# Hybrid mLSTM/attention encoder layer: MLP up product by one level of Strassen's scheme in three token passes, its input made in the attention rounds

## The chip, the cores and the metric

One core of one Trainium2 chip. The metric is the device time of one execution of the whole kernel in microseconds; less is better.

## What is computed

One layer over 2048 prompt tokens and 32 sample tokens, width 1024, in float32: an RMS norm and one input projection that feeds an mLSTM (4 heads, chunk by chunk) and a sliding-window attention (8 query heads); the output projection and the residual; then the MLP, which the change is about; then a gated per-layer embedding and the last norm. Cut to what matters:

```python
x = x + jnp.concatenate([h_m, o_a], axis=-1) @ w_out
x = x + jnp.square(jax.nn.relu(_rmsnorm(x, g_mlp) @ w_up)) @ w_down   # w_up 1024x4096, w_down 4096x1024
x = x + jax.nn.sigmoid(_rmsnorm(x, g_ple) @ w_ple_gate) * (p @ w_ple_proj)
```

In the mLSTM each token needs the running maximum m of its chunk recurrence; every head's row of maxima is spread to all 128 partitions by a product.

## The kernel before

There are 17 tiles of tokens: 16 of 128 and one of 32. Products of full size are made of three matmuls in a reduced float32 type: each operand is split into a high part (a rounding copy, on ACT) and a low part (the remainder, on DVE), and hi*hi, hi*lo and lo*hi are added up in PSUM (split_product, L93; its three matmuls are L98, L99 and L100).

The kernel has three stages. **The mixer** runs mLSTM rounds, one tile a round, and then attention rounds. In both, a round works on several tiles at once, each at another step (r, r-1, r-2), and each engine's program is written out in the order in which it is to run; the engines meet at semaphores. In an mLSTM round PE spreads the maxima by four products with a picking matrix (L565), four products of 4 x 128 by 4 x 128 in plain float32. DVE makes the rows of gates (L716 to L749) and the norm of the tile two rounds ahead. In an attention round PE projects q, k and v, scores, turns the scores, averages, and projects the output; DVE adds it to the residual x_sum (add, L1215 to L1218), and SP stores it as x_mid (L933).

**The MLP** (mlp_phase, L1377) starts after a barrier. It takes the tokens in two halves, of 8 and of 9 tiles. At the start of a half each tile's residual is loaded, squared and summed on ACT (sum_h, L1573), its root taken on POOL (L139, L141), scaled on DVE (scale_h, L1696), turned by 8 transposes on PE (turn_h, L1632) and split (split_h L1580, low_h L1702). The split input of the whole half stays in SBUF. Then 16 blocks of 256 columns of w_up: PE makes the up product in groups of 512 tokens (first half) or 352 (second half), two times 8 chunks of 3 matmuls each; ACT rectifies a group (L1603), DVE squares it (L1735), ACT and DVE split it (L1607, L1739); PE makes the down product, 12 matmuls of 512 columns for each tile, and DVE adds it to the accumulator (L1724). The weights of the next block are loaded by SP into two raw buffers (L1487) and split into a second slot (L1557, L1683) while the block runs: both weight tiles have two slots. The first and the last block of a half are written out, those between run in a hardware loop (blocks).

**The last stage** (ple_phase) is not touched.

Engines take their instructions strictly in order. Which operation stands behind which on ACT's and DVE's queue is so given by the order in the program, and a wait holds all that follows it.

## Time and profile before

| | us |
|---|---|
| median of 3 runs | 2839.81 (2837.72 to 2840.09) |
| profiled execution | 2839.32 |
| its span | 2837.4 |
| mixer, to the start of the MLP | 1018.7 |
| MLP, to the start of the last stage | 1538.9 |

A busy time is the sum of the time in which the engine had an instruction in work; matmuls overlap, and their ends are modelled, so the distance between the starts of two neighbours says more than their durations. PEclk and the granted clock are the share of full speed that TensorE's clock was given.

### The profile page before, as it was taken

The numbers are of one execution on the slowest core, as the hardware profiler recorded it, in microseconds if no ns is written. First come the engines' busy times: TensorE is split into PE (matmuls) and PEld (weight loads), VectorE is DVE, ScalarE is ACT, GpSimd is POOL, SyncE is SP. The second block draws the span as 40 slices with busy tenths as digits, with TensorE's granted clock in tenths as the row PEclk, the third lists the DMA queues.
The fourth block names the chain that finished last, engine by engine and source line by source line (L and its number), as shares of the span: only waits on it lengthen the run. The fifth ranks groups of instructions, "written<-read, shape, count | busy, mean of one in ns | idle before, by whom it ended". The sixth has DMA issues, their size and how long they took to land. (4 is left out here: it accounts for less than half of the span.)

```text
span 2837.4 us, 36654 instructions
## 1 busy us (share of the span) xinstructions
PE 2721.6 (96%) x14337; PEld 2322.3 (82%) x14337; DVE 1372.8 (48%) x2050; ACT 744.9 (26%) x1425; POOL 76.1 (3%) x163
## 2 busy tenths in 40 slices
PE   7999999789999969999999998899999999997998
PEld 6888888678787758888888887798989898985887
DVE  6666565554444444353443545535353535344443
ACT  4333333333333232122121222211111111113232
POOL 0000000000000010000000000000000000000010
PEclk9999999899999989999999999999999999998999
DMA  5121211532222131111111113411111111114221
GB/s 193 55 76 52 73 57 41 152 132 88 81 92 93 47 127 48 50 52 37 59 44 44 58 32 123 130 31 55 34 54 35 52 37 52 37 69 167 84 80 38
DMA packets 90431, 202.93 MB, mean 72 GB/s; under 512 B 9656, under 2 KB 47640, under 8 KB 90360
## 3 DMA queue, kind: packets, MB, share of 16 engines
q1 hardware_dynamic: 89160, 197.63, 21.3%
q0 software_dynamic: 1200, 4.33, 0.5%
q8 instruction: 48, 0.79, 0.1%
q14 instruction: 23, 0.19, 0.0%
HBM read 153.59 MB, written 48.44 MB: 71 GB/s over the span
## 5 line engine op out<-in xcount | busy, mean ns | idle before, releaser
L98 PE MATMUL f_up<-f_hT_hi,f_up_hi 128*128 128x352 f32 (+1 forms) x1280 | 451.9, 353 | 9.8 <-DVE f_hT_lo L1702 9.8
L99 PE MATMUL f_up<-f_hT_lo,f_up_hi 128*128 128x352 f32 (+1 forms) x1280 | 450.8, 352 | 0.0
L100 PE MATMUL f_up<-f_hT_hi,f_up_lo 128*128 128x352 f32 (+1 forms) x1280 | 450.4, 352 | 0.0
L1724 DVE TENSOR_TENSOR f_acc<-f_acc,f_down 128x1024 f32<-128x1024 f32 (+1 forms) x272 | 331.9, 1220 | 223.0 <-PE f_down L100 221.8
L98 PE MATMUL f_down<-f_down_hi,f_uT_hi 128*128 128x512 f32 x1088 | 425.1, 391 | 0.0
L100 PE MATMUL f_down<-f_down_hi,f_uT_lo 128*128 128x512 f32 x1088 | 424.5, 390 | 0.0
L99 PE MATMUL f_down<-f_down_lo,f_uT_hi 128*128 128x512 f32 x1088 | 424.4, 390 | 0.0
L1735 DVE TENSOR_TENSOR f_u<-f_u 128x704 f32<-128x704 f32 (+1 forms) x80 | 82.1, 1026 | 541.3 <-ACT f_u L1603 541.3
L98 PEld LDWEIGHTS f_up<-f_hT_hi,f_up_hi 128*128 128x128 f32 x1280 | 242.0, 189 | 34.3 <-issue 6.6
L1603 ACT ACTIVATE f_u<-f_up 128x704 f32<-128x704 f32 (+1 forms) x80 | 69.3, 866 | 737.2 <-PE f_up L100 737.2
L99 PEld LDWEIGHTS f_up<-f_hT_lo,f_up_hi 128*128 128x128 f32 x1280 | 242.2, 189 | 23.4
L100 PEld LDWEIGHTS f_up<-f_hT_hi,f_up_lo 128*128 128x128 f32 x1280 | 242.4, 189 | 22.6
L100 PEld LDWEIGHTS f_down<-f_down_hi,f_uT_lo 128*128 128x128 f32 x1088 | 204.8, 188 | 43.1
L98 PEld LDWEIGHTS f_down<-f_down_hi,f_uT_hi 128*128 128x128 f32 x1088 | 205.0, 188 | 42.2
L99 PEld LDWEIGHTS f_down<-f_down_lo,f_uT_hi 128*128 128x128 f32 x1088 | 204.8, 188 | 42.3
L1557 ACT ACTIVATE f_down_hi<-f_raw 128x1024 fp32r<-128x1024 f32 x64 | 68.0, 1062 | 319.9 <-DMA f_raw<-in_w_down 319.9
L98 PE MATMUL m_proj<-a_wo_hi,a_mixT_hi 128*128 128x512 f32 x272 | 111.1, 408 | 4.4 <-DVE a_mixT_lo L1185 4.4
L98 PE MATMUL e_gate_ps<-e_wg_hi,e_hT_hi 128*128 128x512 f32 x272 | 109.1, 401 | 3.9 <-DVE e_hT_lo L1963 2.2
L100 PE MATMUL m_proj<-a_wo_hi,a_mixT_lo 128*128 128x512 f32 x272 | 107.0, 393 | 0.0
L99 PE MATMUL e_gate_ps<-e_wg_lo,e_hT_hi 128*128 128x512 f32 x272 | 106.8, 393 | 0.0
L100 PE MATMUL e_gate_ps<-e_wg_hi,e_hT_lo 128*128 128x512 f32 x272 | 106.7, 392 | 0.0
L99 PE MATMUL m_proj<-a_wo_lo,a_mixT_hi 128*128 128x512 f32 x272 | 106.6, 392 | 0.0
(339 smaller groups left out, 4377.2 us busy)
## 6 DMA issues: line engine op xcount, KB each, us to landing
f_raw<-in_w_up SPq DMA_DIRECT2D x64, 512.0 KB, 3.6
f_raw<-in_w_down SPq DMA_DIRECT2D x64, 512.0 KB, 3.5
hT_hi_kept<-m_hT_hi SPq DMA_DIRECT2D x17, 512.0 KB, 4.9
hT_lo_kept<-m_hT_lo SPq DMA_DIRECT2D x17, 512.0 KB, 5.7
a_hT_hi<-hT_hi_kept SPq DMA_DIRECT2D x17, 512.0 KB, 3.6
a_hT_lo<-hT_lo_kept SPq DMA_DIRECT2D x17, 512.0 KB, 4.5
m_x<-in_x_prompt SPq DMA_DIRECT2D x16, 512.0 KB, 4.3
a_x_sum<-in_x_prompt SPq DMA_DIRECT2D x16, 512.0 KB, 3.6
```

Source lines behind the costliest of these rows:

```text
L98: eng.matmul(out, lh(k), rh(k), start=f, stop=False)
L99: eng.matmul(out, lh(k), rl(k), start=False, stop=False)
L100: ins = eng.matmul(out, ll(k), rh(k), start=False, stop=e)
L1557: act.activation(quarter(slot, n, up_hi, down_hi), raw[:, n % 2, :], ACT.Copy).then_inc(w_hi_made, 1)
L1603: act.activation(u[:, :, 0:width], up_ps[g % 2][:, :, 0:width], ACT.Relu).then_inc(rectified, 1)
L1724: dve.tensor_tensor(acc[0:t.n, n, :], acc[0:t.n, n, :], down_ps[n % 2][0:t.n, :], ALU.add).then_inc(added, 1)
L1735: dve.tensor_tensor(part, part, part, ALU.mult).then_inc(squared, 1)
```

## The change

**The up product.** The 4096 columns of w_up are taken as two halves, the 1024 rows as two halves, and the tokens in pairs of tiles. One level of Strassen's scheme (Winograd's form) makes the product of a 2x2 block matrix with another from 7 products of half size where the plain way has 8. A block now takes 128 columns from each half of w_up. Seven products of 4 chunks each are made from seven sums of the weights (or parts) and seven of the input; DVE adds their PSUM results up into the four quarters of the result. Tokens go in three passes: 6, 5 and 6 tiles, in units of two tiles (a lone tile is a unit by its even and odd tokens), with 384, 320 and 336 columns a product. The first block of each pass runs unit by unit (3, 3 and 4 groups), since the operands are made one unit ahead. POOL makes the sums of weights and of inputs, ACT and DVE split all of them. The split weights have one slot each now (up by product, down by half), and the down weights one raw buffer, which both pieces of a block pass through. The result is squared straight from the rectified sum (one instruction) and kept as uT with the two tiles of a unit interleaved, so that the down product reads its stationary at every second column. The down product itself is as before. All weights are loaded three times in place of two.

**The input.** The norm and the turning of a tile move from the MLP's start into the attention rounds, three rounds behind (r-3): ACT squares, POOL takes the root, DVE scales, PE transposes, ACT copies, SP stores the turned tile to memory (hx_kept), and the MLP's POOL queue loads it. One more round follows at the end. The store of x_mid moves behind the round's other DMAs, and the load of the residual comes one round later.

**The maxima.** DVE writes each head's row of maxima on the diagonal of a 4 x 4 x 128 array of zeros, splits it, and PE spreads all four heads with two matmuls of 512 columns in the reduced type (hi and lo, against ones) in place of four in plain float32. Three DVE operations are new (ROW_STEPS 9 to 12).

```diff
-                for h in range(HEADS):
-                    pe.matmul(wide[0:m, h, 0:m], pick[:, h, 0:m], rows[:, U, 0:m], start=True, stop=True)
+                pe.matmul(wide[0:m, :, 0:m], ones_row[:, 0:m], u_hi[:, :, 0:m], start=True, stop=False)
+                pe.matmul(wide[0:m, :, 0:m], ones_row[:, 0:m], u_lo[:, :, 0:m], start=False, stop=True)
...
-                dve.tensor_tensor_scan(rows[:, U, 0:n], zero_row[:, 0:n], rows[:, G, 0:n], m_in, ALU.add, ALU.max).then_inc(row_step, 1)
+                dve.tensor_tensor_scan(rows[:, U, 0:n], rows[:, G, 0:n], rows[:, G, 0:n], m_in, ALU.max, ALU.max).then_inc(row_step, 1)
                 dve.wait_ge(row_step, step + 7)
                 dve.tensor_tensor(m_rows[:, slot, 0:n], rows[:, B, 0:n], rows[:, U, 0:n], ALU.add).then_inc(row_step, 1)
+                dve.tensor_tensor(u_own[:, :, 0:n], pick[:, :, 0:n], rows[:, U, 0:n].unsqueeze(1).to_broadcast([HEADS, HEADS, n]), ALU.mult).then_inc(row_step, 1)
+                dve.wait_ge(row_step, step + 9)
+                dve.tensor_copy(u_hi[:, :, 0:n], u_own[:, :, 0:n]).then_inc(row_step, 1)
+                dve.wait_ge(row_step, step + 10)
+                dve.tensor_tensor(u_lo[:, :, 0:n], u_own[:, :, 0:n], u_hi[:, :, 0:n], ALU.subtract).then_inc(row_step, 1)
...
+            if exists(r - 1):
+                t = tile_at(r - 1, 1 - slot)
+                src = x_sample if t.n < P else x_prompt[token_rows(sp, t.i, P), :]
+                if exists(r - 3):
+                    all_of(sp, x_out, r - 3, 16)
+                    all_of(sp, x_scaled, r - 3)
+                sp.dma_start(x_sum[0:t.n, t.slot, :], src).then_inc(x_sum_in[t.slot], 16)
+            if exists(r - 3):
+                t = tile_at(r - 3, 1 - slot)
+                dst = hx_kept[token_rows(sp, t.i, P), :].rearrange("p (c t) -> p c t", t=P)
+                all_of(sp, hxT_sb, t.i)
+                sp.dma_start(dst[:, :, 0:t.n], hxT[:, :, 0:t.n]).then_inc(hxT_out, 16)
...
+            if exists(done.i):
+                all_of(act, added, done.i, 2)
+                if on_round(r, 3):
+                    act.wait_ge(wo_lo_made, KC)
+                act.activation(hx[0:done.n, :], x_sum[0:done.n, done.slot, :], ACT.Square, scale=D ** -0.5,
+                               accum_out=ms[0:done.n, 0:1]).then_inc(x_squared, 1)
...
+            if exists(done.i):
+                all_of(act, x_turned, done.i)
+                if exists(done.i - 1):
+                    all_of(act, hxT_out, done.i - 1, 16)
+                act.activation(hxT[:, :, 0:done.n], turned[:, :, 0:done.n], ACT.Copy).then_inc(hxT_sb, 1)
...
+        def turn_x(t):
+            all_of(pe, x_scaled, t.i)
+            for c in range(KC):
+                ins = pe.transpose(turned[:, c, 0:t.n], hx[0:t.n, c * P:(c + 1) * P], ident[0:t.n, 0:t.n])
+            ins.then_inc(x_turned, 1)
...
+            if exists(old.i):
+                all_of(pe, mix_lo, old.i, 2)
+            if exists(done.i):
+                turn_x(done)
...
+            if exists(done.i):
+                if on_round(r, 3):
+                    dve.wait_ge(gain_in, 16)
+                all_of(dve, x_rooted, done.i, 2)
+                dve.scalar_tensor_tensor(hx[0:done.n, :], x_sum[0:done.n, done.slot, :], ms[0:done.n, 2:3], gmlp[0:done.n, :],
+                                         ALU.mult, ALU.mult).then_inc(x_scaled, 1)
...
+    UNITS = [[(0, 3), (1, 4), (2, 5)], [(6, 9), (7, 10), (8,)], [(11, 13), (12, 14), (15,), (16,)]]
+    PASSES = range(len(UNITS))
+    B, A, C_, D_ = range(4)
+    BANK = [B, A, C_, D_, A, C_, D_]
+    T2, B11, T3, T1, B21, T4, B22 = range(7)
+    OPERANDS = [B11, T1, T2, B21, B22, T3, T4]
...
+            def load_up(places):
+                for f in (0, 1):
+                    sp.dma_start(up_raw[:, f], w_up[:, places[f]].rearrange("(c p) j -> p c j", p=P)).then_inc(up_in, 16)
...
+            for p in PASSES:
+                def body(b):
+                    g = block_count(p, b)
+                    last = isinstance(b, int) and b == BLOCKS - 1
+                    final = last and p == PASSES[-1]
+                    places, nxt = ([place_of(at, f) for f in (0, 1)] for at in (b, 0 if last else b + 1))
+                    if not final:
+                        reached(sp, up_lo_made, g * 7 + 7)
+                        load_up(nxt)
+                    reached(sp, down_lo_made, g * 2 + 1)
+                    load_down(places[1])
+                    if not final:
+                        reached(sp, down_lo_made, g * 2 + 2)
+                        load_down(nxt[0])
+                    yield
+
+                whole(blocks(sp, p, body))
+                for n, i in enumerate(tiles(p)):
+                    reached(sp, added, down_count(p, BLOCKS - 1, n))
+                    sp.dma_start(x_mlp[token_rows(sp, i, tokens(i)), :], acc[0:tokens(i), n, :]).then_inc(acc_out, 16)
+                sp.wait_ge(acc_out, 16 * sum(len(tiles(n)) for n in range(p + 1)))
+                if p < PASSES[-1]:
+                    load_acc(p + 1)
...
+            def stage(p, u):
+                number, w = units_ahead(p, u), unit_width(UNITS[p][u])
+                a, b = sides(p, u)
+                b11, b12, b21, b22 = by_pair(a[:, 0:HC]), by_pair(b[:, 0:HC]), by_pair(a[:, HC:KC]), by_pair(b[:, HC:KC])
+                pool.wait_ge(h_in[number % 2], h_count(number))
+                reached(pool, op_lo, number * 7)
+                if u == 0:
+                    reached(pool, u_lo, group_count(p, 0) * 4)
+                pool.tensor_tensor(t1_buf(w), b12, b11, ALU.subtract).then_inc(staged, 1)
+                pool.wait_ge(staged, number * 4 + 1)
+                pool.tensor_tensor(t2_buf(w), b22, t1_buf(w), ALU.subtract).then_inc(staged, 1)
+                pool.tensor_tensor(b12, b22, b12, ALU.subtract).then_inc(staged, 1)
+                pool.wait_ge(staged, number * 4 + 2)
+                pool.wait_ge(op_lo, number * 7 + 2)
+                pool.tensor_tensor(t1_buf(w), b21, t2_buf(w), ALU.subtract).then_inc(staged, 1)
+
+            def add_weights(g):
+                a11, a12 = up_raw[:, 0, 0:HC], up_raw[:, 0, HC:KC]
+                a21, a22 = up_raw[:, 1, 0:HC], up_raw[:, 1, HC:KC]
+                reached(pool, up_in, g * 32 + 32)
+                reached(pool, up_lo_made, g * 7)
+                pool.tensor_tensor(sums_sb[:, S1], a21, a22, ALU.add).then_inc(sums, 1)
+                reached(pool, sums, g * 4 + 1)
+                pool.tensor_tensor(sums_sb[:, S2], sums_sb[:, S1], a11, ALU.subtract).then_inc(sums, 1)
+                pool.tensor_tensor(sums_sb[:, S3], a11, a21, ALU.subtract).then_inc(sums, 1)
+                reached(pool, sums, g * 4 + 2)
+                pool.tensor_tensor(sums_sb[:, S4], a12, sums_sb[:, S2], ALU.subtract).then_inc(sums, 1)
...
+            def down_weight_hi(p, b, f):
+                reached(act, down_in, block_count(p, b) * 32 + 16 * f + 16)
+                reached(act, down_done, down_count(p, b, -1))
+                act.activation(down_hi[:, f], down_raw[:], ACT.Copy).then_inc(down_hi_made, 1)
+
+            def u_half(p, k, cols, n):
+                f, side = QUARTERS[n]
+                w = cols.stop - cols.start
+                reached(act, squared, k * 4 + n + 1)
+                act.activation(uT_hi[:, f, cols, side], part[:, PART_OF[n], 0:w], ACT.Copy).then_inc(u_hi, 1)
+
+            def take_p1(k, w):
+                reached(act, product, k * 7 + 2)
+                reached(act, u_lo, k * 4)
+                act.activation(part[:, 0, 0:w], up_ps[A][:, 0:w], ACT.Copy).then_inc(p1_sb, 1)
...
+                    if not first:
+                        down_weight_hi(p, b, 0)
+                    for u, cols in enumerate(groups(p, b)):
+                        k, w = group_count(p, b) + u, cols.stop - cols.start
+                        ahead = operands_hi(p, u + 1) if first and u + 1 < len(UNITS[p]) else iter(range(7))
+                        next(ahead)
+                        next(ahead)
+                        take_p1(k, w)
+                        if first and u == 0:
+                            down_weight_hi(p, b, 0)
+                        if first and u == 1 or not first:
+                            down_weight_hi(p, b, 1)
+                        next(ahead)
+                        next(ahead)
+                        u_half(p, k, cols, 0)
+                        u_half(p, k, cols, 1)
+                        next(ahead)
+                        u_half(p, k, cols, 2)
+                        whole(ahead)
+                        u_half(p, k, cols, 3)
+                    if not last:
+                        for q in range(7):
+                            up_weight_hi(p, b + 1, q)
...
+            def up(p, b, k, cols, u):
+                w = cols.stop - cols.start
+                g = block_count(p, b)
+                if isinstance(b, int) and b == 0:
+                    pe.wait_ge(op_lo, units_ahead(p, u) * 7 + 7)
+                for q, bank in enumerate(BANK):
+                    if u == 0:
+                        reached(pe, up_lo_made, g * 7 + q + 1)
+                    if q == 4:
+                        reached(pe, p1_sb, k + 1)
+                    reached(pe, combined, k * 7 + [-6, -2, -1, 0, 1, 2, 4][q])
+                    split_product(pe, up_ps[bank][:, 0:w], (lambda c: up_hi[:, q, c], lambda c: up_lo[:, q, c]),
+                                  (lambda c: op_hi_sb[:, q, c, cols], lambda c: op_lo_sb[:, q, c, cols]), range(HC)).then_inc(product, 1)
+
+            def down(p, b):
+                k = last_group(p, b)
+                reached(pe, down_lo_made, block_count(p, b) * 2 + 2)
+                for n, i in enumerate(tiles(p)):
+                    reached(pe, u_lo, k * 4 + (3 if place(p, i)[1] == 0 else 4))
+                    reached(pe, added, down_count(p, b, n - 2 if n >= 2 else -1))
+                    for c in range(D // NB):
+                        cols = slice(c * NB, (c + 1) * NB)
+                        ins = split_product(pe, down_ps[n % 2][0:tokens(i), cols],
+                                            (lambda f: stationary(uT_hi, f, p, i), lambda f: stationary(uT_lo, f, p, i)),
+                                            (lambda f: down_hi[:, f, cols], lambda f: down_lo[:, f, cols]), range(2))
+                    ins.then_inc(down_done, 1)
...
+            def combine(w, out, bank, other):
+                dve.tensor_tensor(part[:, out, 0:w], part[:, other, 0:w], up_ps[bank][:, 0:w], ALU.add).then_inc(combined, 1)
+
+            def square(n, w):
+                x = part[:, PART_OF[n], 0:w]
+                dve.scalar_tensor_tensor(x, x, 0.0, x, ALU.max, ALU.mult).then_inc(squared, 1)
+
+            def u_low(k, cols, n):
...
+                    if not first:
+                        down_weight_lo(p, b, 0)
+                    for u, cols in enumerate(groups(p, b)):
+                        k, w = group_count(p, b) + u, cols.stop - cols.start
+                        ahead = operands_lo(p, u + 1) if first and u + 1 < len(UNITS[p]) else iter(range(7))
+                        next(ahead)
+                        next(ahead)
+                        reached(dve, p1_sb, k + 1)
+                        combine(w, 1, B, 0)
+                        if first and u == 0:
+                            down_weight_lo(p, b, 0)
+                        next(ahead)
+                        reached(dve, product, k * 7 + 3)
+                        reached(dve, combined, k * 7 + 1)
+                        combine(w, 2, C_, 1)
+                        if first and u == 1 or not first:
+                            down_weight_lo(p, b, 1)
+                        next(ahead)
+                        reached(dve, product, k * 7 + 4)
+                        reached(dve, combined, k * 7 + 2)
+                        combine(w, 3, D_, 2)
+                        combine(w, 4, D_, 1)
+                        reached(dve, combined, k * 7 + 3)
+                        square(0, w)
+                        u_low(k, cols, 0)
+                        reached(dve, product, k * 7 + 5)
+                        combine(w, 0, A, 0)
+                        reached(dve, combined, k * 7 + 5)
+                        square(1, w)
+                        u_low(k, cols, 1)
+                        next(ahead)
+                        reached(dve, product, k * 7 + 6)
+                        combine(w, 2, C_, 2)
+                        reached(dve, combined, k * 7 + 6)
+                        square(2, w)
+                        u_low(k, cols, 2)
+                        whole(ahead)
+                        reached(dve, product, k * 7 + 7)
+                        reached(dve, combined, k * 7 + 4)
+                        combine(w, 4, D_, 4)
+                        reached(dve, combined, k * 7 + 7)
+                        square(3, w)
+                        u_low(k, cols, 3)
+                    crossing = last and p < PASSES[-1]
+                    ahead = operands_lo(p + 1, 0) if crossing else iter(range(7))
+                    weights = 0
+                    for n, i in enumerate(tiles(p)):
+                        if n == len(tiles(p)) - 1:
+                            while weights < 7 and not (last and not crossing):
+                                up_weight_lo(*((p + 1, 0) if crossing else (p, b + 1)), weights)
+                                weights += 1
+                                if weights > 1:
+                                    next(ahead)
+                            whole(ahead)
+                        add(p, b, n, i)
+                        if n < len(tiles(p)) - 2 and not (last and not crossing):
+                            up_weight_lo(*((p + 1, 0) if crossing else (p, b + 1)), weights)
+                            weights += 1
+                            if weights > 1:
+                                next(ahead)
```

## Rows read from the trace of the kernel before

**Rows 1.** The page, part 1: busy time, share of the span, instructions of each engine.
```profile
PE 2721.6 (96%) x14337; PEld 2322.3 (82%) x14337; DVE 1372.8 (48%) x2050; ACT 744.9 (26%) x1425; POOL 76.1 (3%) x163
```

**Rows 2.** Windows: stretch, length, busy time of each engine, PEclk, DMA share, GB/s.
```profile
60.00:500.00 440.00, 440.00 (x2779) 390.96 (x2778) 271.84 (x633) 158.60 (x400) 22.90 (x29) 1.00 0.18 60
552.00:1000.00 448.00, 430.65 (x2587) 344.39 (x2588) 214.06 (x414) 142.63 (x438) 1.00 (x1) 0.97 0.25 85
1100.00:1740.00 640.00, 640.00 (x2789) 522.91 (x2788) 273.97 (x283) 118.28 (x116) 0.00 (x0) 1.00 0.15 47
1740.00:1790.00 50.00, 37.52 (x175) 31.82 (x174) 30.24 (x30) 18.24 (x25) 10.74 (x20) 0.86 0.61 190
```

**Rows 3.** Timeline of PE, first and last of 57, of 47 and of 23 matmuls.
```profile
1299.84 0.39 PE L98 MATMUL f_down<-f_down_hi,f_uT_hi 128*128 128x512 f32 x1
...
1312.53 0.39 PE L100 MATMUL f_down<-f_down_hi,f_uT_lo 128*128 128x512 f32 x1
...
1999.77 0.32 PE L98 MATMUL f_up<-f_hT_hi,f_up_hi 128*128 128x352 f32 x1
...
2007.09 0.32 PE L99 MATMUL f_up<-f_hT_lo,f_up_hi 128*128 128x352 f32 x1
...
485.95 0.28 PE L99 MATMUL m_proj<-m_og_lo,m_hT_hi 128*128 128x256 f32 x1
...
488.55 0.28 PE L100 MATMUL m_proj<-m_og_hi,m_hT_lo 128*128 128x256 f32 x1
```

**Rows 4.** Timeline of PE: small products in plain float32, several merged into one row.
```profile
484.04 1.06 PE L603 MATMUL m_pair<-m_qkT 128*128 128x128 f32 x8
484.93 1.06 PE L609 MATMUL m_acc<-m_v,m_k 128*128 128x129 f32 x8
...
498.89 1.15 PE L565 MATMUL m_pair<-m_rows,m_pick 4*128 4x128 f32 x8
```

**Rows 5.** Groups of DVE and ACT by shape: busy us, mean ns, idle before.
```profile
L1683 DVE TENSOR_TENSOR f_up_lo<-f_raw,f_up_hi 128x512 fp32r<-128x512 f32 x128 | 87.5, 685 | 0.0
L1224 DVE COPY a_k_twice<-m_proj 128x256 f32<-128x256 f32 x16 | 6.8, 425 | 1.2 <-PE m_proj L100 0.3
L985 ACT ACTIVATE a_wq_hi<-a_wq_raw 128x512 fp32r<-128x512 f32 x8 | 4.4, 617 | 0.0
L992 ACT ACTIVATE a_wkv_hi<-a_wkv_raw 128x256 fp32r<-128x256 f32 x8 | 2.5, 398 | 0.0
```

**Rows 6.** Timeline of a steady MLP block: DVE's square and the ACT operation that waits for it.
```profile
1341.72 1.23 DVE L1735 TENSOR_TENSOR f_u<-f_u 128x1024 f32<-128x1024 f32 x1 [7.49 <-ACT f_u L1603]
...
1343.06 1.06 ACT L1607 ACTIVATE f_uT_hi<-f_u 128x1024 fp32r<-128x1024 f32 x1 [1.37 <-DVE f_u L1735]
```

**Rows 7.** DMA issues with us to landing; a window with one such load in it.
```profile
f_raw<-in_w_up SPq DMA_DIRECT2D x64, 512.0 KB, 3.6
f_raw<-in_w_down SPq DMA_DIRECT2D x64, 512.0 KB, 3.5
...
1349.00:1353.00 4.00, 4.00 (x20) 3.30 (x19) 3.10 (x4) 1.06 (x1) 0.00 (x0) 1.00 0.38 131
```

**Rows 8.** Timeline: the MLP's start and end; and one POOL group of 128 elements.
```profile
1018.67 0.20 POOL L148 MEMSET f_ident<- 128x128 f32 x1 [465.06 <-POOLq L1310]
...
2557.59 0.35 SPq L1816 DMA_DIRECT2D e_x<-x_after_mlp  x1
...
L150 POOL TENSOR_SCALAR_AFFINE_SELECT f_ident<-f_ident 128x128 f32<-128x128 f32 x1 | 0.3, 294 | 0.1
```

**Rows 9.** Timeline of PE: first product, and transposes, after idle times of different length.
```profile
1044.11 0.77 PE L98 MATMUL f_up<-f_hT_hi,f_up_hi 128*128 128x512 f32 x1 [6.20 <-DVE f_hT_lo L1702]
...
1047.65 0.40 PE L100 MATMUL f_up<-f_hT_hi,f_up_lo 128*128 128x512 f32 x1
...
1771.94 1.94 PE L1632 MATMUL f_up<-f_ident,f_h 128*128 128x128 f32 x8 [3.20 <-DVE f_h L1696]
...
1783.00 1.07 PE L1632 MATMUL f_down<-f_ident,f_u 128*128 128x128 f32 x8 [2.12 <-DVE f_u L1696]
```

605 lines of the change are left out of this document (259 added, 346 removed).

## The prediction

> **What bounds the kernel now.** I read the page first: PE is busy for 96% of the span, DVE for 48%, ACT for 26%, POOL for 3% [rows 1]. Then the table of windows, for the stages that the change touches: in an mLSTM stretch of 440 us PE is busy for all of it, in the attention rounds for 430.7 of 448, in the steady MLP blocks of the first half for all of 640 us [rows 2]. So PE's issue rate sets the time in all three, and whatever shortens PE's queue is worth its own length, as long as no other engine becomes late. Last the timeline, for what one matmul costs in a row of many. The mean durations of the groups overlap and don't serve; starts do. 56 intervals of 512 columns take 12.69 us, 0.2266 each; 46 of 352 take 7.32, 0.159 each; 22 of 256 take 2.60, 0.118 each [rows 3]. That is a line: 0.010 us plus 0.000423 us a column. It gives 0.172 for 384 columns, 0.145 for 320 and 0.152 for 336, the widths of the three passes.
>
> The profiled execution took 2839.32 us, span 2837.4; the median of the runs is 2839.81. My sum is made against 2839.3.
>
> **Term 1, the up product in full groups: -83.** Before, per block 96 matmuls of 512 and, in the second half, 144 of 352: 16 x (96 x 0.2266 + 144 x 0.159) = 714 us. After, per block 7 products x 12 matmuls = 84: 16 x 84 x (0.172 + 0.145 + 0.152) = 631 us.
>
> **Term 2, the down product: 0.** 12 matmuls of 512 columns for each of 17 tiles in 16 blocks, before and after: 740 us. Its stationary is now read at every second column. No row has that; weight loads sit at 0.111 us each where they bind [rows 4], so even at double cost they fit beneath 0.2266.
>
> **Term 3, the first block of each pass: +84.** There the groups are one unit (128 columns or less): 3 + 3 + 4 = 10 groups of 84 matmuls. The nearest rows are 128-wide fp32 instructions, 8 in 0.89 us, 0.111 each [rows 4]; lower bound 0.064 from the line above, upper 0.222 (a plain fp32 product of 128 columns takes two such instructions). I take 0.111: 9.3 us a group. In the same time DVE has 7 operand remainders (512 elements, 0.6 from start to start), 14 operations of 128 elements (about 0.29) and 1.2 of down weights, 9.5 us, and waits for ACT in between; so 12 us a group. From pass 2 on the second piece of the down weights also stands behind 3 MB of accumulator tiles on SP's queue. I take 124 us for the three blocks, where the widths of term 1 hold 14.5 + 12.2 + 12.8 = 39.5. At 0.064 DVE and ACT hold it anyway (-17); at 0.222 it grows by about 65.
>
> **Term 4, a new wait in each of the 45 later blocks: +168.** This decides. Before, one rectify, one square and one split of up to 1024 elements followed a group, and other groups' matmuls covered them. Now, for 384 columns, DVE has 7 additions, 4 squares and 4 splits, ACT 5 copies, in one order. Prices: DVE 256 elements 0.425, 512 0.685, so 0.555 for 384; ACT 0.398 and 0.617, so 0.51 [rows 5]. DVE to ACT and back costs 0.14 (idle 1.37 around an operation of 1.23) [rows 6]. Let T be the start of the block's first product in pass 1; one product takes 12 x 0.172 = 2.07, the seventh ends at T+14.5.
> - ACT converts the first down piece once the last down matmul is through, T+0.2 to 1.3. DVE first adds the last tile (to 1.7), then takes the remainder, to 2.8.
> - Only then does SP issue the load of the second piece into the same buffer. Alone it lands in 3.5 us; 512 KB take 1.6 us of the queues (131 GB/s over 4 us), and 1 MB of next up weights, issued at T+0.6, is ahead [rows 7]. It lands at about 7.6 (6.4 without them).
> - ACT 7.7 to 8.7; DVE's remainder 8.8 to 10.0. The fourth product was ready at 8.4; its additions stand behind this in DVE's queue.
> - Then 10 DVE operations (4 additions, 3 squares, 3 splits; 5.6), three ACT copies between square and split (1.5) and their hand-overs (0.4), less 0.4 where DVE operations overlap: 7.1. Done at 17.1.
> The first down tile needs that split: PE waits 17.1 - 14.5 = 2.6. Pass 2 has a shorter cover (12.2), only three weight remainders between its tiles so that the last addition is 0.6 later, 10 operations of 0.48: done at 16.9, wait 4.7. Pass 3: 16.5 - 12.8 = 3.7. 15 x (2.6 + 4.7 + 3.8) = 168. Bounds: with the second piece there in time, DVE could start at the fourth product (8.4, 7.1, 7.5) and the waits are 1.3, 1.6 and 1.5, 66 us; with 512-byte packets at half the byte rate the load is 3.2 us later, +144. I stay near the first figure: the queues carry the old 1 KB packets and 4 KB packets in the same 3.5 to 3.6 us, so bytes, not packets, seem to set the time, and I add a tenth.
>
> **Term 5, what stood around the MLP: -53.** Before, the MLP started at 1018.7 and its first product at 1044.1, 25.4 later [rows 8, 9]. After: the attention part ends with one more tail (square 1.24, POOL 0.75, scale 1.28, transposes 0.9, copy 0.4, store 2.0 for 32 rows, one behind the other): +5 in the mixer, in term 6. From the start of the MLP both up pieces and two tiles load (5 us), POOL makes 4 weight sums and 4 operands (no row for 512 elements; its 128-element row of 0.294 times 4 gives 1.2 each), ACT and DVE split 14 pieces: 20.5 us to the first product. -5. From the first product to the start of the next stage it was 1513.5, of which 1454 are the matmuls of terms 1 and 2: 59.5 for 13 tiles' transposes, the idle of the half boundary (12.5 of 50 us) and the end [rows 2, 8]. After, two crossings at 3 to 4 us (operands are made beside the last down product) and an end of 4: 11. -48.
>
> **Term 6, the mixer: +12.** Attention: 8 transposes a tile more on PE, 0.9 and a hand-over, 17 x 0.95 = +16. Their helpers (ACT +2.3 us a round, DVE 1.3, POOL 0.8, SP a store of 512 KB) are covered by a round of 27 us in which DVE and ACT are under half busy [rows 2]; SP's new waits stand ahead of loads that are two rounds early. If that cover fails it is 17 x 2.3 = 39. mLSTM: 8 instructions of about 1.0 us (1.15 to the end of the last) [rows 4] become two of 0.227: 17 x -0.54 = -9. DVE gets three operations of 512 elements more, 2 us a round at 62% busy [rows 2]: nothing, or 34 if it is late. The longer tail: +5.
>
> **Term 7, the clock: +20.** After PE idled for 3.20 us eight transposes took 1.94, after 2.12 us 1.07; the MLP's first 8 matmuls, after 6.20 us, took 3.54 to the ninth where 8 intervals are 1.81 [rows 9]: the lower of the clock's two levels, 1.2 GHz, and a loss of 1.7. The waits of passes 2 and 3 are long enough; I take half of 30 blocks at about 1.4.
>
> Sum: -83 + 84 + 168 - 53 + 12 + 20 = +148, so 2987. Some 0.2% (6 us) is what a measurement of this kernel can tell from nothing.
>
> **A rule against the change.** POOL now adds SBUF operands four times a block, about from T+6 to T+11, beside DVE's squares and splits; in the trace POOL does no such work, so no row bears on it. The Trainium skill, "SBUF — State Buffer" (section "SBUF: two separate sides"), says that DVE with two SBUF inputs and GpSimd share a port pair that one holds for its whole instruction while the other waits. By that rule every remainder, square and split could stand up to 1.2 us behind POOL.
>
> **Rivals.**
> - No waits, faster: ACT and DVE keep up, as the 48% and 26% suggest, and the down weights land in time. From term 4's wait below 0.5 us a block on. Then 2839.3 - 83 + 84 - 53 + 12 = 2799. For it: 15 us of DVE's work lie beside 30 of PE. Against it: even the bound with everything loaded leaves 66 us. 0.12.
> - Waits of about 1 us a block, +44 in term 4: 2843, no change. 0.03.
> - POOL and DVE exclude each other: one operation of 1.2 us in the way of the chain in each of 45 blocks, and the clock lost oftener, and some 5 us in the first groups: +80, 3067. 0.23.
> - 128-wide products at 0.222: 3052. 0.10.
> - My own sum, 2930 to 3040: 0.48. Several of the bad ends together, 3150: 0.04.
> The low end, 2860, is term 4 at its bound of 66 us with no loss of clock (2865); the high end is the port's case with slow packets. Left out of 2860 to 3110 are the faster case, the unchanged one and the last: 0.19. Faster 0.12, same 0.03, slower 0.85; the slower cases' own range is 2920 to 3110.
>
> **What would show it.** In the profile after: matmuls of 384 columns starting 0.172 apart; PE idle before the first down matmul of each block, ended by the DVE split, for 2.6, 4.7 and 3.7 us; blocks of 33.4, 30.5 and 32.8 us; DVE idle before the first addition behind the down piece's remainder, ended by ACT and that by the DMA; first blocks of 36, 39 and 49 us of up product. Blocks of 31, 26 and 29 us would refute term 4. A granted clock below 1 in passes 2 and 3 and not in pass 1 bears out term 7. A POOL addition of much more than 1.2 us, or DVE splits that last longer while POOL runs, would speak for the port.

## The result, and the profile after

The kernel after takes 3217.98 us (median of 4 runs, 3209.45 to 3220.23) where the kernel before, run beside it, takes 2839.95: a ratio of 1.1326 (95% interval 1.1309 to 1.1343). The forecast was 2987, its range 2860 to 3110. Slower was right; the size was not. In the profiled executions the span grew by 370.2 us, from 2837.4 to 3207.6, where I had summed up 148.

The page, part 1 and the row of TensorE's clock, after:

```profile
PE 2885.8 (90%) x15015; PEld 2490.5 (78%) x15015; DVE 1832.5 (57%) x2992; ACT 910.4 (28%) x1914; POOL 423.4 (13%) x401
...
PEclk9999998999999599999996999999679998998999
```

PE is no longer busy all the time (96% before [rows 1]), POOL works for 423 us where it had 76, and the clock has three holes, of 5, 6 and 6 to 7 tenths, where the three passes begin.

Windows of the kernel after: the up product of the three first blocks, then the later blocks of passes 1, 2 and 3 (length, busy time and count of PE, PEld, DVE, ACT, POOL, granted clock, DMA share, GB/s):

```profile
1061.11:1116.12 55.01, 54.35 (x253) 53.97 (x253) 28.15 (x59) 13.04 (x29) 19.62 (x18) 0.50 0.28 96
1693.26:1745.38 52.12, 51.79 (x253) 51.60 (x253) 25.64 (x59) 11.39 (x29) 17.30 (x17) 0.52 0.44 152
2277.70:2350.00 72.30, 71.97 (x337) 71.78 (x337) 27.27 (x81) 13.49 (x41) 16.40 (x18) 0.50 0.26 84
1153.74:1673.35 519.61, 468.81 (x2184) 416.98 (x2185) 314.81 (x421) 118.14 (x196) 89.39 (x56) 0.93 0.19 57
1761.65:2258.05 496.40, 411.51 (x2102) 363.84 (x2100) 297.56 (x424) 118.14 (x202) 94.53 (x60) 0.94 0.21 63
2368.84:2905.58 536.74, 469.84 (x2269) 398.33 (x2268) 315.70 (x437) 119.23 (x202) 88.60 (x56) 0.92 0.19 56
```

In the first three rows PE is hardly ever idle and yet issues a matmul of 128 columns or fewer only every 0.213 us, at a granted clock of 0.50 (the level of 1.2 GHz) from beginning to end, but for the first 2.5 us of the second row. In the other three the count times the spacing at full clock falls short of the length: there PE waits, and the clock is below 1 for some of the time. Where it waits stands in the groups by shape:

```profile
L97 PE MATMUL f_down<-f_down_hi,f_uT_hi 128*128 128x512 f32 x1024 | 447.2, 437 | 178.0 <-DVE f_uT_lo L1823 168.5 <-issue 9.5
L97 PE MATMUL f_up<-f_op_hi,f_up_hi 128*128 128x320 f32 x420 | 131.9, 314 | 23.5 <-DVE f_part L1813 23.5
L97 PE MATMUL f_up<-f_op_hi,f_up_hi 128*128 128x128 f32 x196 | 80.7, 412 | 38.2 <-DVE f_op_lo L1801 38.2
```

The first wait is term 4's, ended by the DVE split as foretold. The second lies inside the up product of pass 2, ahead of its seventh product, for a PSUM bank that DVE has still to read (1.57 us a block). The third belongs to the first blocks, most of it to the start of the MLP (30.2 us). Now one block of pass 1 in the timeline; its up product starts at T = 1433.29:

```profile
1441.32 1.06 ACT L1701 ACTIVATE f_down_hi<-f_down_raw 128x1024 fp32r<-128x1024 f32 x1 [3.07 <-DMA f_down_raw<-in_w_down]
1442.41 1.55 DVE L1810 TENSOR_TENSOR f_down_lo<-f_down_raw,f_down_hi 128x1024 fp32r<-128x1024 f32 x1 [2.01 <-ACT f_down_hi L1701]
1442.84 2.28 POOL L1652 TENSOR_TENSOR f_sums<-f_up_raw 128x512 f32<-128x512 f32 x1
1443.89 1.01 DVE L1813 TENSOR_TENSOR f_part<-f_part,f_up 128x384 f32<-128x384 f32 x2
1444.82 0.71 DVE L1817 SCALAR_TENSOR_TENSOR f_part<-f_part 128x384 f32<-128x384 f32 x1
1445.08 1.60 POOL L1654 TENSOR_TENSOR f_sums<-f_up_raw,f_sums 128x512 f32<-128x512 f32 x1
1446.15 0.95 DVE L1823 TENSOR_TENSOR f_uT_lo<-f_part,f_uT_hi 128x384 fp32r<-128x384 f32 x1 [0.62 <-ACT f_uT_hi L1707]
...
1447.60 0.56 DVE L1817 SCALAR_TENSOR_TENSOR f_part<-f_part 128x384 f32<-128x384 f32 x1
1448.77 0.56 DVE L1823 TENSOR_TENSOR f_uT_lo<-f_part,f_uT_hi 128x384 fp32r<-128x384 f32 x1 [0.61 <-ACT f_uT_hi L1707]
...
1451.68 0.79 PE L97 MATMUL f_down<-f_down_hi,f_uT_hi 128*128 128x512 f32 x1 [3.64 <-DVE f_uT_lo L1823]
1452.27 0.63 PE L98 MATMUL f_down<-f_down_lo,f_uT_hi 128*128 128x512 f32 x1
1452.70 0.63 PE L99 MATMUL f_down<-f_down_hi,f_uT_lo 128*128 128x512 f32 x1
```

Three things are to be seen. ACT takes the second down piece at T+8.0, as it lands (7.6 was reckoned). The three DVE operations that lie beside POOL's additions take 1.55, 0.71 and 0.95 us where the same operations alone take 1.22, 0.56 and 0.56, and a POOL addition of 1.29 takes 2.28; the DVE additions, which read PSUM, are not longer. And after the wait of 3.64 us the down matmuls start 0.43 apart, not 0.233, some ten of them; in the whole MLP about 450. That isn't so behind every such wait. One block later the wait is as long, and nothing is lost:

```profile
1489.29 0.50 PE L97 MATMUL f_down<-f_down_hi,f_uT_hi 128*128 128x512 f32 x1 [3.63 <-DVE f_uT_lo L1823]
1489.63 0.39 PE L98 MATMUL f_down<-f_down_lo,f_uT_hi 128*128 128x512 f32 x1
```

Of the 45 waits 41 are followed by slow down matmuls and four are not: two of 3.60 and 3.63 us, and those of the last blocks of passes 1 and 3 (3.30 and 2.14).

**The account**, term by term, forecast against measured in the trace (the counts and spacings are those of the timeline; a crossing is PE's idle time between two passes):

| term | forecast | measured | how |
|---|---|---|---|
| 1 full groups, spacing | -83 | -79 | 0.1736, 0.1453, 0.1536 a matmul |
| 2 down product | 0 | +18 | 0.2333 for 0.2266, for 14 of 17 tiles |
| 3 first blocks | +84 | +140 | 55.0 + 52.1 + 72.3 = 179.4, not 124 |
| 4 waits in 45 blocks | +168 | +226 | 277 + 277 + 267 of up product, less 595 at full rate |
| 5 around the MLP | -53 | -48 | first product 26.2 after the start, not 20.5; crossings and end as reckoned |
| 6 mixer | +12 | +16 | MLP starts at 1034.9, not 1018.7 |
| 7 clock | +20 | +96 | down product 861, less 740, 18 of term 2 and 7 of crossings |

The sum is 369; the other 1.6 of the 370.2 lie in the last stage. The mixer's end is 1034.9 here and lies between 1035.0 and 1040.7 in the profiles of the nine runs below that leave the mixer of the kernel after as it is, so term 6 is known to a few us only. Terms 3, 4 and 7 are to be explained; the experiments take them up.

### The profile page after: what moved, and what is told of

Read it like the earlier page. It is cut to its first block and busy times, and to the rows that moved or that the text cites. A ratio compares the mean times of both kernels' runs of the same rounds, so it can differ in the third digit from the quotient of the medians.

```text
span 3207.6 us, 42512 instructions
## 1 busy us (share of the span) xinstructions
PE 2885.8 (90%) x15015; PEld 2490.5 (78%) x15015; DVE 1832.5 (57%) x2992; ACT 910.4 (28%) x1914; POOL 423.4 (13%) x401
## 5 line engine op out<-in xcount | busy, mean ns | idle before, releaser
L97 PE MATMUL f_down<-f_down_hi,f_uT_hi 128*128 128x512 f32 (+1 forms) x1088 | 472.5, 434 | 178.0 <-DVE f_uT_lo L1823 168.5
L97 PE MATMUL f_up<-f_op_hi,f_up_hi 128*128 128x384 f32 (+5 forms) x1540 | 519.7, 337 | 67.2 <-DVE f_op_lo L1801 38.2
L98 PE MATMUL f_up<-f_op_lo,f_up_hi 128*128 128x384 f32 (+5 forms) x1540 | 516.7, 336 | 0.0
L99 PE MATMUL f_up<-f_op_hi,f_up_lo 128*128 128x384 f32 (+5 forms) x1540 | 516.6, 335 | 0.0
L98 PE MATMUL f_down<-f_down_lo,f_uT_hi 128*128 128x512 f32 (+1 forms) x1088 | 464.3, 427 | 0.0
L99 PE MATMUL f_down<-f_down_hi,f_uT_lo 128*128 128x512 f32 (+1 forms) x1088 | 462.1, 425 | 0.0
L97 PEld LDWEIGHTS f_down<-f_down_hi,f_uT_hi 128*128 128x128 f32 (+1 forms) x1088 | 227.0, 209 | 244.2 <-issue 190.7
L97 PEld LDWEIGHTS f_up<-f_op_hi,f_up_hi 128*128 128x128 f32 x1540 | 329.0, 214 | 80.1 <-DVE f_op_lo L1801 39.9
L98 PEld LDWEIGHTS f_up<-f_op_lo,f_up_hi 128*128 128x128 f32 x1540 | 329.4, 214 | 2.0
L99 PEld LDWEIGHTS f_up<-f_op_hi,f_up_lo 128*128 128x128 f32 x1540 | 329.5, 214 | 0.0
```

What stands on the lines that cost most here:

```text
L97: eng.matmul(out, lh(k), rh(k), start=f, stop=False)
L98: eng.matmul(out, lh(k), rl(k), start=False, stop=False)
L99: ins = eng.matmul(out, ll(k), rh(k), start=False, stop=e)
```

## The experiments

All but runs 1 and 7 are edits of the kernel after.

**1. Prices alone.** A kernel that computes nothing of the reference: trains of matmuls and of vector operations, executed once.

> Leaves out the whole computation: it runs trains of matmuls of the kernel's form and vector operations of its forms, to price them alone. (a) Width of the moving operand, 36 matmuls each from 512 down to 64 columns. Theory: the spacing follows 0.010 us + 0.000423 a column down to at least 320 (0.145), and below some width between 320 and 128 it stands at 0.213, whatever the width. Rival: the line goes on (0.118 at 256, 0.064 at 128), and the 0.213 of the changed kernel comes from something around its first blocks. (b) Stationary at every second column. Theory: 0.233 at 512 columns where the plain one has 0.227. Rival: 0.227 for both, and the 0.233 comes from reads that other engines share. (c) Vector operations beside POOL additions of 512 elements. Theory (one port pair for two SBUF inputs): a subtraction or a square of two SBUF inputs takes up to 1.3 us more, an addition with one input in PSUM and a copy stay as they are; an addition on POOL of 1.3 us alone reaches 2.2. Rival: nothing changes, or all forms slow down alike. (d) PE idle for 1 to 10 vector operations of 0.7 us and then 60 matmuls. Theory: after about 2 us nothing is lost, after 3.6 us and more some 12 matmuls come at 0.43 in place of 0.227, a loss of 2.4 us. Rival: a gradual loss from the first idle on.

DVE's operations, three of each form, first alone, then while POOL adds without a pause; and POOL's additions beside DVE (18) and alone (6):

```profile
10.77 2.14 DVE L134 TENSOR_TENSOR t_out<-t_a,t_b 128x512 fp32r<-128x512 f32 x3 [0.63 <-PE t_dve_bank L104]
...
16.72 1.75 DVE L138 SCALAR_TENSOR_TENSOR t_same<-t_same 128x384 f32<-128x384 f32 x3
18.50 1.73 DVE L140 TENSOR_TENSOR t_same<-t_a,t_dve_bank 128x384 f32<-128x384 f32 x3
20.27 1.15 DVE L142 COPY t_same<-t_a 128x384 f32<-128x384 f32 x3
...
23.37 5.15 DVE L134 TENSOR_TENSOR t_out<-t_a,t_b 128x512 fp32r<-128x512 f32 x3 [1.74 <-POOL t_mk L177]
...
35.25 4.67 DVE L138 SCALAR_TENSOR_TENSOR t_same<-t_same 128x384 f32<-128x384 f32 x3
39.96 1.73 DVE L140 TENSOR_TENSOR t_same<-t_a,t_dve_bank 128x384 f32<-128x384 f32 x3
41.72 3.55 DVE L142 COPY t_same<-t_a 128x384 f32<-128x384 f32 x3
...
23.29 28.14 POOL L171 TENSOR_TENSOR t_pout<-t_pa,t_pb 128x512 f32<-128x512 f32 x18
...
62.92 7.51 POOL L171 TENSOR_TENSOR t_pout<-t_pa,t_pb 128x512 f32<-128x512 f32 x6 [11.23 <-DVE t_chain L150]
```

A subtraction of two SBUF inputs goes from 0.71 to 1.72 us each, a square from 0.58 to 1.56, a plain copy from 0.38 to 1.18, an addition with one input in PSUM stays at 0.58; POOL's goes from 1.25 to 1.56. That is the theory, but for the copy, which it held to be safe. By the Trainium skill, "SBUF — State Buffer", section "SBUF: two separate sides", a DVE operation with two SBUF inputs, or one in a fast mode, and a POOL operation that reads SBUF shut each other out for their whole length. These rows agree: 0.71 us alone becomes 1.72 beside additions of 1.25, and the copy is held up like the others.

PE, 36 matmuls at each width (the first number behind the bar is the length of the train), and 60 matmuls after an idle time of 0.85, 2.96, 3.69 and 4.42 us:

```profile
L99 PE MATMUL t_bank<-t_mv,t_st 128*128 128x256 f32 x36 | 4.5, 283 | 0.0
L99 PE MATMUL t_bank<-t_mv,t_st 128*128 128x192 f32 x36 | 4.2, 273 | 0.0
L99 PE MATMUL t_bank<-t_mv,t_st 128*128 128x128 f32 x36 | 4.2, 274 | 0.0
L99 PE MATMUL t_bank<-t_mv,t_st 128*128 128x64 f32 x36 | 6.1, 341 | 0.0
...
119.92 13.90 PE L99 MATMUL t_bank<-t_mv,t_st 128*128 128x512 f32 x60 [0.85 <-DVE t_chain L159]
...
168.32 13.94 PE L99 MATMUL t_bank<-t_mv,t_st 128*128 128x512 f32 x60 [2.96 <-DVE t_chain L159]
185.94 15.54 PE L99 MATMUL t_bank<-t_mv,t_st 128*128 128x512 f32 x60 [3.69 <-DVE t_chain L159]
205.90 16.45 PE L99 MATMUL t_bank<-t_mv,t_st 128*128 128x512 f32 x60 [4.42 <-DVE t_chain L159]
```

At the full clock 128 columns cost 0.111 (starts in the timeline), as I had priced them, and 192 and 240 cost the same. Both of the ideas on width fall: there is no step up to 0.213 (the theory), and no line down to 0.064 (its rival). Within the train of 64 columns the clock fell to 0.50, and only from there on the spacing was 0.213. So 0.213 is the floor of 0.111 at the lower clock. The train with its stationary at every second column has 36 intervals in 8.40 us, 0.2333, the plain one 8.16, 0.2266: the stride costs 0.0067 there, and nothing at 384 columns (0.174 with and without). And an idle time of up to 2.96 us cost nothing, 3.69 cost 1.6 us, 4.42 cost 2.5, 5.87 cost 1.7 and 7.32 cost 2.2. Here that is a step and not a slope; each length stood once in this run, and runs 3, 9 and 10 have shorter waits that cost something.

**2. The wait filled.**

```diff
                 reached(pe, down_lo_made, block_count(p, b) * 2 + 2)
+                w = all_cols(p).stop
+                for _ in range(0 if isinstance(b, int) and b == 0 else (20, 26, 26)[p]):
+                    pe.matmul(up_ps[B][:, 0:w], down_hi[:, 0, 0:P], down_lo[:, 0, 0:w], start=True, stop=True)
```

> In the 45 later blocks PE runs 20, 26 or 26 extra matmuls (pass 1, 2, 3) into a free bank between the seventh up product and the first down matmul, 3.5 to 4.0 us that fit into the wait of 3.8 to 4.3 us; nothing that is computed changes. Theory (the wait costs twice: once as idle time, once as a lower clock in the down matmuls behind it): the down matmuls go back from 0.260 to 0.233 on average, 2.0 to 2.3 us a block, so about 90 us less in all, 3128, with the first down matmul where it was. Rival (the slower down matmuls have another cause, such as their stationary or reads shared with DVE): 3218 or a little more.

3126.87 us, ratio 1.101 (1.0984 to 1.1036): 91 less, by work that does nothing. The later blocks of pass 1, a granted clock of 0.93 before:

```profile
1156.35:1675.00 518.65, 512.83 (x2556) 465.64 (x2556) 335.17 (x445) 127.65 (x213) 99.00 (x63) 1.00 0.20 63
```

The first down matmul comes at T+18.5 as before; the down product takes 85 us less, and about 25 of its matmuls start 0.43 apart where 450 did. That the waits bring the lower clock is shown, and its size: 85 of the 96 us of term 7.

**3 and 9. POOL's sums made small; POOL's sums made later.** Run 3 cuts the four additions to a sixteenth; run 9 keeps them and puts one wait ahead:

```diff
+                        reached(pool, u_lo, last_group(p, b) * 4 + 3)
                         add_weights(block_count(p, b) + 1)
```

> POOL's four weight additions of a block are cut from 512 to 32 elements in all blocks but the first (leaves out the sums of the up weights there, so the up product is wrong). Theory (POOL and DVE keep each other out when both read SBUF twice): the remainder of the second down piece goes from 1.55 to 1.22 us, the first square from 0.71-0.76 to 0.5-0.56, the first split from 0.95 to 0.5-0.56, so the chain ends 0.9 to 1.0 us earlier and the first down matmul comes at T+17.4 in place of 18.4: 45 x 1.0 = 45 us less, 3173. Rival (those three are longer for another reason): the same time.

> POOL makes the weight sums of the next block only once three quarters of this block's hidden values are split (about T+18), beside the down product, and no longer beside the squares and splits; nothing that is computed changes. Theory (it is where POOL's four additions lie, not that they are made, that costs the 49 us of the small sums): the chain shortens as there, the first down matmul comes at T+17.4 to 17.5, and ACT has all seven up pieces long before the block ends: 45 x 1.0 less, 3170. Rival (moved there they hold up DVE's remainders of the next up weights, which the next block waits for): no gain, 3200 or more.

3168.66 (ratio 1.1162, 1.1135 to 1.1190) and 3172.23 (1.1176, 1.1157 to 1.1195), 49 and 46 less than 3217.98. The up product's part of the 45 blocks is 45 us shorter in both (776 for 821), the first down matmul comes at T+17.5. DVE's splits of 384 elements, after and in run 3:

```profile
L1823 DVE TENSOR_TENSOR f_uT_lo<-f_part,f_uT_hi 128x384 fp32r<-128x384 f32 x60 | 39.4, 657 | 36.9 <-ACT f_uT_hi L1707 36.9
```

```profile
L1824 DVE TENSOR_TENSOR f_uT_lo<-f_part,f_uT_hi 128x384 fp32r<-128x384 f32 x60 | 33.6, 560 | 36.9 <-ACT f_uT_hi L1708 36.9
```

So POOL costs 1.0 us a block by where its additions lie (run 9 moves them by some 10 us), not by being there. What POOL doesn't cost is the clock. The waits ahead of the first down matmul are 2.8, 3.45 and 3.45 us on average (passes 1, 2 and 3) in both runs, where they were 3.7, 4.1 and 4.1, and yet the down product takes 861.7 and 863.5 us where it took 860.9: as many of its matmuls (459 and 462) start 0.43 apart. What is left, T+17.5, 17.4 and 16.8, is within 0.5 of my chain (17.1, 16.9, 16.5).

**4. The tiles of a unit side by side.**

```diff
-        uT_hi, uT_lo = sb("uT_hi", [P, 2, WIDTH, 2], F32R), sb("uT_lo", [P, 2, WIDTH, 2], F32R)
+        uT_hi, uT_lo = sb("uT_hi", [P, 2, 2, WIDTH], F32R), sb("uT_lo", [P, 2, 2, WIDTH], F32R)
```

> The two tiles of a unit lie one behind the other in the stationary of the down product, not at every second column (leaves out the down product of the four tiles that have no partner: they take another unit's columns). Theory: the stationary with a stride costs 0.0067 us a matmul, 13 x 16 x 12 x 0.0067 = 17 us, so 3201; down matmuls at full clock start 0.2266 apart. Rival: no change, 3218, and the spacing stays 0.233.

3210.48, ratio 1.1300 (1.1274 to 1.1326), 7.5 less and not separable from the kernel after by its interval. The spacing did go back to 0.2266 (the first down product of pass 1 takes 17.59 us for 18.12), but in this profile the clock was lost for longer behind the waits of pass 1: 203 of its down matmuls are slow, where 134 were. The size of the stride is taken from the spacings of runs 1 and 4; 14 tiles have a partner (three have none, not four as the expectation says), so it is 14 x 16 x 12 x 0.0067 = 18 us. The total doesn't show it.

**5. The first blocks at full width.** The operands of all units come first, then one group:

```diff
-            return [unit_cols(p, u) for u in range(len(UNITS[p]))] if isinstance(b, int) and b == 0 else [all_cols(p)]
+            return [all_cols(p)]
...
-                        ahead = operands_lo(p, u + 1) if first and u + 1 < len(UNITS[p]) else iter(range(7))
+                        for unit in range(1, len(UNITS[p]) if first else 0):
+                            whole(operands_lo(p, unit))
+                        ahead = iter(range(7))
```

> The first block of each pass makes the operands of all its units first and then runs its up product once at full width (384, 320, 336 columns), as the later blocks do; nothing that is computed changes. Theory (the 128-wide groups cost 0.213 a matmul at the lower clock, 55.0 + 52.1 + 72.3 = 179 us of up product, and full width holds the clock): PE starts some 11, 11 and 17 us later (5.5 us of DVE and ACT for each further unit), then needs 18.5 us to the first down matmul: 3 x 18.5 + 39 = 95, so 85 us less, 3133. Rival (the making of the operands bounds the first block, as my term 3 had it, with 12 us a group): 10 groups x 12 of operand work stay and 3 x 14 come behind them, so about 160 in place of 179, 3200.

3157.93, ratio 1.1120 (1.1099 to 1.1140): 60 less, not 85. A further unit takes 9.8 us (DVE has its seventh remainder of the first at 1062.5, of the third at 1082.0), not 5.5, since POOL's four additions and DVE's remainders shut each other out there too, and the group starts at the lower clock (17.6 us for 14.4 from the first start to the last).

**6. A warm start.**

```diff
+                    for _ in range(36 if isinstance(b, int) and b == 0 and u == 0 and q == 0 else 0):
+                        pe.matmul(up_ps[B][:], up_hi[:, 0, 0], up_hi[:, 0].rearrange("p c j -> p (c j)"), start=True, stop=True)
```

> Ahead of the first 128-wide group of each pass PE runs 36 extra matmuls of 512 columns into a free bank (10.6 us, the first 12 of them at the lower clock); nothing that is computed changes. Theory (the lower clock is what makes a 128-wide matmul cost 0.213, and a start at the full clock holds it for a while): the first group after the extra matmuls runs at 0.111, 9.3 us in place of 18, and where DVE's operands are late behind it PE waits and falls back; so 8.7 us are won and 10.6 are spent in each pass, about the same total, 3224, with a granted clock of 1.0 in that group. Rival (128 columns cost 0.213 with these operands at any clock): the group keeps its 18 us and the total is 32 us more, 3250.

3224.53, ratio 1.1356 (1.1338 to 1.1374). The extra matmuls, the first group and the rest of the first block in pass 1:

```profile
1061.50:1071.80 10.30, 9.57 (x36) 7.84 (x37) 3.10 (x5) 0.63 (x1) 7.48 (x6) 0.82 0.53 148
1071.90:1081.20 9.30, 9.30 (x85) 9.30 (x83) 4.59 (x12) 3.36 (x7) 0.00 (x0) 1.00 0.33 113
1081.20:1121.20 40.00, 36.29 (x170) 35.95 (x170) 20.96 (x44) 9.06 (x22) 12.19 (x12) 0.51 0.19 66
```

The same group of 84 matmuls takes 9.3 us at a clock of 1.00 and 18 at 0.50. Behind it PE waits 3.7 us for the next operands, so that a group takes 13.0 us even at full clock; then the clock is gone and stays gone through 40 us of narrow matmuls.

**7. The maxima alone**, in the kernel before.

> The kernel before with the change of the mLSTM maxima alone (two matmuls over the split diagonal in place of four fp32 ones). Theory: 8 small instructions of about 1.0 us become two of 0.227 in each of 17 rounds, DVE's three additional operations a round are covered: 9 us less, 2831. Rival: PE waits for the longer chain of DVE's row steps, up to 2 us a round, 34 us more, 2874.

2833.92 beside 2839.99, ratio 0.9980 (0.9970 to 0.9991): faster by 6 us, clear of noise but small, and the one version of this study that beats both kernels. The mLSTM part ends 5.5 us earlier in the trace (the attention part's first operation on POOL at 520.1, not 525.6), so of the mixer's +16.2 the attention part has +21.7 (forecast +16 and +5) and the mLSTM part -5.5 (forecast -9).

**8 and 10. The chain mended.** Run 8 has run 5's edit and two more, run 10 also run 9's:

```diff
-                    if not final:
-                        reached(sp, up_lo_made, g * 7 + 7)
-                        load_up(nxt)
                     reached(sp, down_lo_made, g * 2 + 1)
                     load_down(places[1])
+                    if not final:
+                        reached(sp, up_lo_made, g * 7 + 7)
+                        load_up(nxt)
...
                         square(0, w)
-                        u_low(k, cols, 0)
                         reached(dve, product, k * 7 + 5)
                         combine(w, 0, A, 0)
+                        u_low(k, cols, 0)
```

(and the same for the quarter behind it)

> Three edits together, all of which leave the results as they are: the first blocks at full width; the second piece of the down weights loaded ahead of the next up weights; and on DVE the next quarter's addition stands between a square and its split, so that it runs while ACT copies. Theory: the first edit is worth 85 us; the second lets the second piece land 1.6 us earlier; the third takes two gaps of 0.6 us out of the chain to the first down tile, so the wait goes from 3.8, 6.3 and 5.2 us a block to about 1.0, 3.5 and 2.4, 126 us, and where it is below 3 us the clock holds, another 30 to 90 us: 3218 - 85 - 126 - 60 = 2947. Rival (another queue is late next, such as POOL's sums for the next up weights behind the later load): less than 60 us for the second and third edit, 3075 or more.

> The kernel of all three mended places (whole first blocks, second down piece first, additions between square and split) with POOL's sums moved beside the down product; nothing that is computed changes. Theory (in the run before this the earlier chain only ran into POOL's later sums: squares of 1.64 us for 0.56, splits of 0.92): without them the chain goes 9.1 (remainder), 10.0, 10.5, 11.1, 12.2, 13.1, 13.4, 14.0, 15.2, so the first down matmul comes at T+15.3, 15.2 and 14.7 where it was 18.2 to 18.5; 48 blocks x 3.3 = 158 less, and the waits of 0.7 to 3 us leave the clock up, another 90: 3165 - 158 - 90 = 2917. Rival (the two reorderings are worth nothing by themselves, the wait has yet another cause): 3165 less the 49 of the sums, 3116.

Run 8: 3165.02, ratio 1.1141 (1.1125 to 1.1158), 7 more than run 5 (in the profiles 5.7 of that lie in the mixer, which the edits don't touch): the theory falls, its rival holds. Run 10: 2940.48, ratio 1.0358 (1.0341 to 1.0375), 225 less than run 8 by one wait on POOL. A block of pass 1 in run 8, and the same operations in run 10:

```profile
1401.84 0.92 DVE L1821 TENSOR_TENSOR f_uT_lo<-f_part,f_uT_hi 128x384 fp32r<-128x384 f32 x1
1402.68 1.64 DVE L1815 SCALAR_TENSOR_TENSOR f_part<-f_part 128x384 f32<-128x384 f32 x1
...
1401.05 1.30 POOL L1646 TENSOR_TENSOR f_sums<-f_up_raw 128x512 f32<-128x512 f32 x1 [31.45 <-DMA f_up_raw<-in_w_up]
1402.42 1.49 POOL L1648 TENSOR_TENSOR f_sums<-f_sums,f_up_raw 128x512 f32<-128x512 f32 x1
```

```profile
1359.00 0.55 DVE L1822 TENSOR_TENSOR f_uT_lo<-f_part,f_uT_hi 128x384 fp32r<-128x384 f32 x1
1359.46 0.55 DVE L1816 SCALAR_TENSOR_TENSOR f_part<-f_part 128x384 f32<-128x384 f32 x1
...
1363.40 0.50 PE L97 MATMUL f_down<-f_down_hi,f_uT_hi 128*128 128x512 f32 x1 [0.75 <-DVE f_uT_lo L1822]
```

In run 8 the second piece lands 1.3 us and DVE's chain begins 1.6 us earlier than in the kernel after, and POOL's additions, which wait for the up weights, begin 3.4 us later: they now lie on three quarters' squares and splits (up to 1.64 us for 0.55), and the gain is eaten. With them out of the way the first down matmul comes at T+15.5, 14.9 and 14.5. The expectation had 2917; the waits are as reckoned, but in pass 2 PE idles for 2.36 us and the clock still falls, for some eight down matmuls in 13 of its 15 later blocks; in the other two the same wait costs nothing.

**11. The clock kept**, run 10 with two fillings as in runs 2 and 6.

> The kernel of the run before (2940) with two fillings of PE's waits; nothing that is computed changes: in the later blocks of pass 2 14 extra matmuls of 320 columns (2.0 us) ahead of the first down matmul, where PE waits 2.4 us and 8 of its down matmuls then come at 0.43; and in the first block of each pass 30 extra matmuls of 512 columns (9 to 10 us) while the last unit's operands are made, so that its up product begins at the full clock. Theory (a wait's second price is the clock): 1.5 us for each of 15 blocks and 3.4 to 6.7 us in each first block, 22 + 17 = 39 less, 2901. Rival (the slow stretches are those of the work itself, not of the wait ahead of it): no gain, 2940 or more.

2924.93, ratio 1.0309 (1.0292 to 1.0326), 15.5 less, not 39. The down product of pass 2 gains 16.7 us, 1.1 a block. The first groups of passes 2 and 3 are 4 us shorter each, but the waits behind them grow by 1.3 to 1.4 us, and eight slow down matmuls follow each (1.5 us); that of pass 1 gains nothing. In pass 3 the filling itself is in the way:

```profile
2123.07 9.46 PE L1765 MATMUL f_up<-f_up_hi 128*128 128x512 f32 x30 [23.54 <-DVE f_op_lo L1808]
2132.36 0.31 PE L97 MATMUL f_up<-f_op_hi,f_up_hi 128*128 128x336 f32 x1
...
2126.30 0.21 DVE L1808 TENSOR_TENSOR f_op_lo<-f_part,f_op_hi 128x64 fp32r<-128x64 f32 x1
```

The last unit there is the tile of 32 tokens, and its operands are done at 2126.5. The 30 extra matmuls run until 2132.36 and hold the group up by 5.8 us. Against the kernel before, beside which it ran (2836.79), 88 us remain: the first groups come 20 us and more after the end of the pass before, and the attention part is dearer.

## Why the prediction was right and wrong

**The sign, and what carried it.** The forecast rested on the wait ahead of the first down tile, and that came, at its place and from its cause: ended by DVE's split, behind a second down piece that is loaded late. The product's gain was within 4 us of term 1, terms 5 and 6 within 5, though term 6 is the sum of two misses: the mLSTM part gained 5.5 and not 9, the attention part cost 21.7 and not 21.

**Term 4, mis-sized: +168, measured +226.** 45 of the 58 are POOL's additions lying on DVE's remainder, square and split (runs 3, 9). I had the place and the rule and a price of 1.2 us a block, near the 1.0 that was measured, but left it to a rival at 0.23 instead of putting it into the sum. The rule of the Trainium skill ("SBUF — State Buffer", section "SBUF: two separate sides") speaks of the very pair of operations that the change brings together; no row spoke against it. That is the error of judgement. Both signs that I had named for it came: a POOL addition of 2.28 us and DVE splits of 0.95. (The sum 15 x (2.6 + 4.7 + 3.8) is 166.5, not 168; that slip is small.)

**Term 7, the largest miss: +20, measured +96.** The step that failed is "half of 30 blocks at about 1.4". I left pass 1 out, since its wait was to be 2.6 us, and halved the rest. In the kernel after, the waits of all three passes come to 3.7 us and more on average, and in 41 of the 45 blocks about ten matmuls at double price follow, 2.1 us a block over all 45. POOL's part in the waits isn't the reason: without it pass 1 waits 2.8 us, near my 2.6, and some six down matmuls a block are still slow, and the loss of all three passes together is the same (runs 3, 9). My own sign for the term, a clock below 1 in passes 2 and 3 but not in pass 1, failed too: 0.93, 0.94 and 0.92. The trace of before shows nothing lost after 2.12 us and a loss after 3.20 [rows 9]; run 1 puts 2.96 us on the free side, run 10 has 2.36 on the other. My waits of 4.7 and 3.7 us lay beyond the 3.20 that had cost something, and the 2.6 between the two rows: to halve the first and leave out the second had no row behind it. What decides whether one wait is followed by the lower clock stays open. The Trainium skill, "TensorE: Matmul & The Clock Gate", section "Part 1: The HAM clock gate (the "warmup" mystery)", has the clock halved after idleness and released by activity; the trace agrees for 41 of the 45 waits.

**Term 3, mis-sized: +84, measured +140.** 0.111 a matmul was the right price at the full clock, and 12 us a group near what the operands would have allowed (9.3 and a wait of 3.7 in run 6). The step left out the clock: in pass 1 PE comes from 30 us of idleness at the lower one, and over these narrow matmuls, though PE is busy for 54.35 of 55.01 us, it doesn't rise. The rival "128-wide at 0.222" had the time, for a reason (two instructions each) that run 6 refutes: the same 84 matmuls take 9.3 us there. By the same section of the Trainium skill the clock follows how busy PE has been, which would have had it rise here if busy meant what the profile counts. It stayed at 0.50, and the measurement decides.

**Term 2: 0, measured +18.** A stationary at every second column isn't hidden behind a matmul of 512 columns: 0.0067 us each.

The measured result lies beyond even "several of the bad ends together" (3150, at 0.04), since three terms missed to the same side, by 56 (first blocks), 58 (waits) and 76 us (clock). That isn't POOL making the waits long enough for the clock to fall: in the kernel after, they cost as much clock without its part (runs 3, 9). Only in the mended chain do the two go together: with POOL out of the way, run 10's waits of 0.75 us in pass 1 and 1.5 us in pass 3 cost no clock.

## What to carry to other kernels

Price a wait of the busiest engine twice: as its length, and as the half speed behind it wherever waits of about its length have been followed by the lower clock in some trace; here that was so from 2.36 us on, and it cost 2.1 us a block. Where a change hands work to POOL, look for which DVE operations with two SBUF inputs will lie beside it, and put that into the sum; here moving four additions out of its way was worth 46 us alone and 225 once the rest of the chain was short. See at which clock a stretch of narrow matmuls begins: from the lower one it didn't rise here. And where extra matmuls fill a wait, see that they end before it does; run 11's did not in pass 3.
